# Bias rows of two MLPs in two fp32r parts inside the down passes, and attention heads begun inside the projections

## What is computed

```python
# MLP of the first block (width 4096, squared ReLU)
y = square(relu(h @ w1 + b1)) @ w2 + b2
# LRU mixer's last step
m = (h * gelu(yb)) @ w_out + b_out
# both attentions, 8 heads of 128 (+64 rotary in the first)
s = q @ k.T * scale + bias_or_mask
p = exp(s - max(s)) / sum(exp(s - max(s)))
o = p @ v
```

## Time and profile before

| | us |
|---|---|
| median of 3 runs | 1750.84 (1749.12 to 1753.19) |
| the profiled execution | 1750.2 |
| its span | 1748.6 |
| PE busy | 1646.2 (94%) |
| DVE busy | 1147.3 (66%) |
| ACT busy | 839.1 (48%) |
| POOL busy | 153.8 (9%) |
| chain that ended last, share of PE | 71% |
| the same, share of DVE | 16% |

### The profile page before, as it was taken

One profiled execution on the slowest core, in us unless ns is written; L12 is line 12 of the kernel. 1 busy time (PEld: TensorE's weight loads), 2 busy tenths in 40 slices (PEclk: granted clock), 3 DMA queues, 4 the chain that ended last, 5 costly groups with the idle time before them and its releaser, 6 DMA issues.

```text
span 1748.6 us, 20517 instructions
## 1 busy us (share of the span) xinstructions
PE 1646.2 (94%) x8221; PEld 1327.7 (76%) x8221; DVE 1147.3 (66%) x1354; ACT 839.1 (48%) x1134; POOL 153.8 (9%) x293
## 2 busy tenths in 40 slices
PE   7778999988988999999999999999999999799998
PEld 3656787875677788878888868888788888578887
DVE  4699778888969665575546876544754546665554
ACT  3553465544234555544335875334634435553433
POOL 4510100026600100000000000000000000000000
PEclk9878999999999999999999989999999999899999
DMA  9838588752036566445654554555555554245551
GB/s 305 310 126 308 185 302 332 288 214 100 1 142 220 193 227 238 161 168 192 225 184 141 199 189 171 192 192 169 207 178 183 186 188 167 96 144 193 193 191 74
DMA packets 145096, 335.45 MB, mean 192 GB/s; under 512 B 18213, under 2 KB 34061, under 8 KB 143850
## 3 DMA queue, kind: packets, MB, share of 16 engines
q1 hardware_dynamic: 134310, 293.65, 48.8%
q0 software_dynamic: 9696, 37.29, 5.6%
q10 hardware_dynamic: 996, 3.20, 0.5%
HBM read 328.86 MB, written 6.83 MB: 192 GB/s over the span
## 4 chain that ended last, share of the span: by engine, by line
PE 71%; DVE 16%; ACT 5%; issue 4%; POOL 2%; DMA 1%; SPq 1%; DVEq 0%; ACTq 0%; POOLq 0%
PE ps L670 22%; PE ps L672 22%; PE ps L671 22%; DVE wlo L1794 3%; PE ps L755 2%; ACT whi L1253 1%; DMA operands<-in_mod_mix_w 1%; PE ps L749 1%; DVE work L2247 1%; DVE xlo L1799 1%; PE ps L762 1%; DVE B L1927 1%; POOL mod L2509 1%; DVE B L1926 1%; DVE small L1859 1%
## 5 line engine op out<-in xcount | busy, mean ns | idle before, releaser
L1794 DVE TENSOR_TENSOR wlo<-raw,whi 128x2048 fp32r<-128x2048 f32 (+2 forms) x247 | 559.8, 2283 | 253.5 <-ACT whi L1253 252.2
L1253 ACT ACTIVATE whi<-raw 128x2048 fp32r<-128x2048 f32 (+2 forms) x247 | 466.9, 1908 | 233.9 <-PE ps L672 170.5
L670 PE MATMUL ps<-whi,xhi 128*128 128x512 f32 (+2 forms) x1244 | 477.5, 384 | 18.9 <-DVE xlo L1799 17.3
L672 PE MATMUL ps<-whi,xlo 128*128 128x512 f32 (+2 forms) x1244 | 471.8, 379 | 0.0
L671 PE MATMUL ps<-wlo,xhi 128*128 128x512 f32 (+2 forms) x1244 | 471.7, 379 | 0.0
L670 PE MATMUL ps<-whi,hhi 128*128 128x512 f32 x736 | 294.6, 400 | 6.2 <-DVE hlo L1799 5.2
L671 PE MATMUL ps<-wlo,hhi 128*128 128x512 f32 x736 | 289.0, 393 | 0.0
L672 PE MATMUL ps<-whi,hlo 128*128 128x512 f32 x736 | 288.8, 392 | 0.0
L670 PEld LDWEIGHTS ps<-whi,xhi 128*128 128x128 f32 x1244 | 235.5, 189 | 64.6 <-DVE xlo L1799 21.0
L672 PEld LDWEIGHTS ps<-whi,xlo 128*128 128x128 f32 x1244 | 235.5, 189 | 44.2
L671 PEld LDWEIGHTS ps<-wlo,xhi 128*128 128x128 f32 x1244 | 235.8, 190 | 41.7
(11 more groups left out here) (371 smaller groups left out, 1599.8 us busy)
## 6 DMA issues: line engine op xcount, KB each, us to landing
raw<-in_mlp_w SPq DMA_DIRECT2D x64, 1024.0 KB, 5.6
raw<-in_ffn_w_gate SPq DMA_DIRECT2D x44, 1024.0 KB, 5.1
raw<-in_ffn_w_up SPq DMA_DIRECT2D x44, 1024.0 KB, 5.2
raw<-in_ffn_w_down SPq DMA_DIRECT2D x44, 1024.0 KB, 4.9
mod<-in_mod_ffn_w POOLq DMA_DIRECT2D x16, 1024.0 KB, 6.9
mod<-in_mod_mix_w POOLq DMA_DIRECT2D x12, 1024.0 KB, 7.4
operands<-in_mod_mix_w SPq DMA_DIRECT2D x8, 1024.0 KB, 8.5
raw<-in_lru_w_in SPq DMA_DIRECT2D x8, 1024.0 KB, 5.2
```

Source lines behind the costliest of these rows:

```text
L670: pe.matmul(o, lh, rh, start=start, stop=False)
L672: return pe.matmul(o, ll, rh, start=False, stop=stop)
L1253: act.activation(whi[:, c % SPL, 0:n], raw[:, c % RAW, 0:n], ACT.Copy).then_inc(hi_done, 1)
L1794: dve.tensor_tensor(wlo[:, c % RAW, 0:n], raw[:, c % RAW, 0:n], whi[:, c % SPL, 0:n].bitcast(F32), ALU.subtract).then_inc(lo_done, 1)
```

## The change

- **MLP bias rows.** ScalarE rounds the bias row to fp32r (`brow_hi`) between `hi(c+4)` and `hi(c+5)`, VectorE makes the rest (`brow_lo`) between `lo(c+4)` and `lo(c+5)`. `open_acc` is no longer called in the MLPs: the first down pass of each token half issues, for each of its two banks, two fp32r matmuls of one row (high and low part) ahead of the first product. They come after the wait for `hid_ok`.
- **LRU.** `open_acc("lru")` stands ahead of `turned(3)` instead of behind it.
- **First attention.** Group 0's rotary transposes stand inside the projection of group 1, group 1's after the scores of head 0; the loop starts on `q_ok` 2 and `qt_ok` 1, and the waits for all of them move to i = 1. ScalarE does `hi(5)` between the two rotary copies.
- **Second attention.** The scores of heads 0 to 2 stand inside the last projection passes; ScalarE's feature copies of slice 0 go ahead of `hi(c+5)`, `hi(c+6)` between the two token copies; VectorE's `lo(c+6)` moves behind the first head.
- **Softmax weights.** In both attentions VectorE gives only the reciprocal (`recips`, signal `rc_ok`); ScalarE multiplies the weights in place, two Copy activations with a scale column, after the exponential of the next head, and gives `p_ok`.

```diff
             def down(c, tile, tt, first=False, final=False, src=(hhi, hlo), biased=None):
 ...
                     for n in range(2):
+                        if biased and k == 0:
+                            half = slice(512 * n, 512 * (n + 1))
+                            pe.matmul(ps[:, 2 * tt + n, :], ones_r[0:1, :], brow_hi[:, half], start=True, stop=False)
+                            last = pe.matmul(ps[:, 2 * tt + n, :], ones_r[0:1, :], brow_lo[biased][:, half], start=False, stop=False)
+                            if tt and n:
+                                last.then_inc(acc_open, 1)
 ...
-                    if i == 0:
-                        open_acc(name)
                     for tt in range(T):
+                        if i == 0:
+                            acc_ready(name, tt)
+                            pe.wait_ge(brow_lo_ok, MLPS.index(name) + 1)
                         pe.wait_ge(hid_ok, HID0[name] + 2 * i + tt + 1)
-                        down(mlp_down(name, i, 0), 4 * (i % 2), tt)
+                        down(mlp_down(name, i, 0), 4 * (i % 2), tt, biased=name if i == 0 else None)
 ...
                 sliced(3, 1, 9)
-                turned(3)
                 pe.wait_ge(lg_ok, KT)
                 open_acc("lru")
+                turned(3)
 ...
+                    if g:
+                        turn_rotary(0)
 ...
-                pe.wait_ge(q_ok, 4)
-                pe.wait_ge(qt_ok, 2)
+                pe.wait_ge(q_ok, 2)
+                pe.wait_ge(qt_ok, 1)
                 attention(0, qT, kT, V, True)
 ...
             def beside_attention(i):
+                if i == 0:
+                    turn_rotary(1)
                 if i == 1:
+                    pe.wait_ge(q_ok, 4)
+                    pe.wait_ge(qt_ok, 2)
                     same_step()
 ...
                 hi(c + 4)
+                if l == 0:
+                    act.activation(ones_r[:, :], ones[0:1, :], ACT.Copy)
+                act.wait_ge(brow_in, 16 * (l + 1))
+                act.activation(brow_hi[:, :], brow[name], ACT.Copy).then_inc(brow_hi_ok, 1)
                 hi(c + 5)
 ...
+                    if 1 <= i <= HEADS:
+                        s = (i - 1) % 3
+                        act.wait_ge(rc_ok, HEADS * n + i)
+                        for tt, (lo, up) in enumerate(((0, P), (P, 3 * P))):
+                            last = act.activation(sms[:, s, lo:up], sms[:, s, lo:up], ACT.Copy, scale=recips[:, 2 * s + tt:2 * s + tt + 1])
+                        last.then_inc(p_ok, 1)
 ...
                     lo(c + j)
+                    if j == 4:
+                        dve.wait_ge(brow_hi_ok, MLPS.index(name) + 1)
+                        rest(brow_lo[name][:, :], brow[name], brow_hi[:, :]).then_inc(brow_lo_ok, 1)
 ...
-                        do(dve.reciprocal(newton[:, 0:2], atts[:, 2 * s:2 * s + 2]))
-                        dve.tensor_scalar(sms[:, s, 0:P], sms[:, s, 0:P], newton[:, 0:1], None, ALU.mult)
-                        dve.tensor_scalar(sms[:, s, P:3 * P], sms[:, s, P:3 * P], newton[:, 1:2], None, ALU.mult).then_inc(p_ok, 1)
-                        dve.wait_ge(p_ok, e + 1)
+                        dve.reciprocal(recips[:, 2 * s:2 * s + 2], atts[:, 2 * s:2 * s + 2]).then_inc(rc_ok, 1)
 ...
                 c = FIRST["att"]
                 for tt in range(T):
                     token_turn("att", 0, tt)
-                for tt in range(T):
-                    project("att", c + 3, slice_bank(1, tt), tt, 1)
+                project("att", c + 3, slice_bank(1, 0), 0, 1)
+                acc_ready("att", 1)
+                pe.wait_ge(feat_ok, FEAT0["att"] + 2)
+                scores(1, 0, qT2, kT2, False)
+                scores(1, 1, qT2, kT2, False)
+                project("att", c + 3, slice_bank(1, 1), 1, 1)
+                scores(1, 2, qT2, kT2, False)
```

More of the change, by code:

```diff
@@ L965, in mla, with turn_rotary @@
                 spread_third(1, (6, 7))
+            def turn_rotary(g):
+                pe.wait_ge(qp_ok, g + 1)
+                for r in range(2):
+                    for tt in range(T):
+                        last = pe.transpose(ps[:, 4 * g + 3, r * L + tt * P:r * L + (tt + 1) * P], qp_tok[:, g, tt, r * P:(r + 1) * P], ident[:, :])
+                last.then_inc(qt_ps, 1)
             def z_pass(c, tt):
@@ L2187, in attention @@
                         piece(6)
+                    if n and i == 0:
+                        lo(FIRST["att"] + 6)
             def s5():
@@ L2361, in att @@
                 c = FIRST["att"]
-                for j in range(3, 7):
+                for j in range(3, 6):
                     lo(c + j)
```

61 lines of the change are left out of this document (34 added, 27 removed).

## The result

| | us |
|---|---|
| before, median of 4 runs | 1751.3 (1749.12 to 1753.19) |
| after, median of 4 runs | 1769.2 (1768.51 to 1771.42) |
| ratio after / before | 1.0107, 95% interval 1.0092 to 1.0123 |
| the profiled executions: before, after | 1750.2, 1768.5 |
| their spans | 1748.6, 1766.7 |

The change costs 18 us. The forecast was 1756.3, range 1749.5 to 1761.5: the sign is right, the loss is three times the forecast one, and outside the range.

The account below looks back on a forecast made before the run. TensorE, busy 94% of the span, was taken as the bound. MLPs +6.1, LRU +0.5, first attention -1.4, second +1.2, less 0.3 for slack, gave +6.1 on 1750.2: 1756.3 us, range 1749.5 to 1761.5.

Parts of the forecast that it names:

- VectorE's extra instruction: MLP starts: one more VectorE instruction for the bias row, ahead of residual, makes hid_ok come 1.22 us later.
- Idle time of 5.7: MLP starts: TensorE's idle time before the first down pass grows from 0.8 to about 5.7 us.
- LRU: LRU end: fourth down pass at most 1.4 us earlier, half clock after the wait costs 1.9; +0.5 us.
- Second attention: Second attention: ScalarE's copies lengthen the period to about 3.97 us, early scores give some back; +1.2 us.
- First attention: First attention: VectorE saves 0.6 us a head, GpSimd's slower chain costs 0.7; -1.4 us in all.
- the MLP term: Both MLP starts: later hid_ok plus bias matmuls now behind the wait, +3.04 us each, +6.1 for both.
- The price of the bias matmuls: MLP starts: eight bias matmuls each, 0.23 us apart at full clock, add 1.82 us to TensorE's path.
- The half clock: MLP starts: half clock after TensorE's restart stays at 5.8 and 2.9 us, no change, ±1.5 for each.
- One-row matmuls lower the clock: Rival, MLPs: one-row matmuls cause the half clock, so down passes start at full clock; 1752.0 us, chance 0.14.
- Early starts arrive: Rival, first attention and LRU: waits end earlier than assumed, 5.4 and 7.2 us gained; 1743.7 us, chance 0.08.
- ScalarE the bound: Rival, both attentions: ScalarE's copies cost 0.75 us and also stand in the way in the first; 1761.3 us, chance 0.12.
- GpSimd shut out: Rival, first attention: VectorE's pieces hold GpSimd's chain, memset and head 3 about 3 us later; 1758.6 us, chance 0.11.

Follow-up runs that it names:

- run 3: Changed kernel with the eight fp32r bias matmuls of each MLP moved ahead of the wait for hid_ok; 1759.49 us.
- run 6: Changed kernel with the MLP starts as before the change and the softmax weights multiplied on VectorE again in both attentions; 1754.09 us.
- run 4: Changed kernel without the eight bias matmuls of each MLP, the rounding of the bias row and the wait for it kept; 1760.61 us.
- run 5: Changed kernel with the eight one-row bias matmuls of each MLP replaced in place by eight matmuls of 128 rows; 1762.07 us.
- run 9: Changed kernel with 24 full matmuls added ahead of the first wait for hid_ok in each MLP, where TensorE idled; 1759.07 us.
- run 2: Kernel before with the MLP part of the change alone; 1765.3 us.
- 12: The combined kernel of 11 with the eight bias matmuls of each MLP back inside the passes, residual still late; 1746.2 us.
- run 1: Changed kernel with the MLP starts as before (fp32 bias matmuls ahead of the wait, no bias rounding); 1754.89 us.
- run 10: Kernel before with only VectorE's residual moved behind the two hidden steps of slice 0, bias matmuls still fp32; 1747.53 us.
- run 8: Kernel before with MLP bias rows in two fp32r parts ahead of the wait and VectorE's residual behind the hidden steps of slice 0; 1744.21 us.
- 11: Combined kernel: late residual, split bias rows ahead, first attention as changed, second with early scores but scaling on VectorE, old LRU order; 1741.55 us.
- run 7: Kernel before with only the LRU's open_acc moved ahead of the last eight transposes; 1751.22 us.

## Why the prediction was right in its sign and wrong in its size

**What held.** VectorE's extra instruction: +1.22 forecast, the gap grew by 1.30 and 1.33. Idle time of 5.7: measured 5.75 and 5.78. That the old fp32 rows were hidden and give nothing back: run 3, which hides them again, recovers 10 us. LRU: +0.5 forecast, +1.6 measured, with the wait for `hg_lo` 2 (5.11) and the half clock behind it as described. From the last projection matmul the fourth pass comes 1.4 earlier (22.51 in place of 23.87), as summed; the half clock of 6.1 us behind it costs 3.0 where the sum had 1.9. It lies at the sum's upper bound. Second attention: +1.2 forecast, +2.1 measured, period 3.97 forecast and 3.98 to 3.99 measured; the pair of copies was put at 0.6 and takes 0.69 from start to next start (1518.86 to 1519.55). Run 6 shows that all of the loss is the scaling. First attention: -1.4 forecast. It starts 0.3 later and ends 0.4 earlier in the profiled executions, -0.7. GpSimd's memset came 1.5 later in the stage where the sum had 0.7, and the scaling on ScalarE is worth about 3 (run 6), not 2.15. That the terms nearly cancel is partly luck: this stage's length varies by more than 0.7 with the same code.

**What failed: the MLP term.** The prediction put it at +3.04 each, +6.1 for both; the windows give +8.8 and +7.0, beyond its upper bound of +4.5 too. The wait of 1.22 in it was right; two steps were wrong.

- The price of the bias matmuls: "8 for each MLP, 0.23 us apart at full clock", 1.82 us. The rate was taken from products of 128 rows; at full clock the eight cost 3.3, since a change between one row and 128 slows two steps by 0.1 each. Missing: 1.5 for each, 3.0 in all. The trace of before had a hint that was passed over: from the last projection matmul (194.33) to the first bias row (194.65) it is 0.32, not 0.23.
- The half clock: "I take the same stretches after the restart, no change". Measured: 7.0 and 3.7 lost in place of 2.8 and 1.4, +6.5 in all. This is the bigger error, and it has a cause that runs 4, 5 and 9 isolate: after the same idle time the half clock costs 2.0 to 2.6 with products of 128 rows alone (four starts, runs 4 and 5) and 3.4 to 7.0 with eight single rows among them (four starts, after and run 2); with the wait filled or 0.6 to 0.8 us long it costs nothing (9, 12). Here the idle time starts it and the single rows draw it out. The medians agree in direction and give smaller sizes: after lies 8.6 us over run 4 and 7.1 over run 5, and less the bias matmuls' price (6.6, and 3.0 over 128 rows) that leaves 2.0 and 4.1 for the longer half clock.

Sum for both MLPs: 2.6 (gap) + 6.6 (bias matmuls) + 6.5 (half clock) = 15.7, against 15.8 in the windows. The stages grew by 14.4, so 1.4 is regained later in them, where the prediction took off 0.3 for slack. The half clock's part is the least certain: in run 2 the same code lost 3.8 and 3.4, 3.0 more than before in place of 6.5. By the medians the MLP part costs 13.4 (run 2 against before) to 14.3 (after against run 1).

**The range** allowed +4.5 for each MLP "if the half clock lasts longer" but did not carry both MLPs' upper ends into 1761.5, and no row set that upper end.

**The rivals.** *One-row matmuls lower the clock*: its mechanism is borne out (run 10, and the kernel before, whose clock fell ahead of the 0.8 us of waiting), its consequence was drawn the wrong way. It asked what happens when the one-row matmuls go, but the change did not remove them, it moved them to where TensorE has just restarted. The test it named, first down matmuls 0.23 apart, came out against it. *Early starts arrive*: no; both waits end where the prediction put them. *ScalarE the bound*: in the second attention only, run 6. *GpSimd shut out*: the memset came 1.5 later, between the 0.7 of the sum and the 3 of the lock. By the rule of the Trainium skill, "SBUF — State Buffer", § Who interferes with whom, the loser of the shared port stands still for the whole of the other's instruction; the rows show both slowed, a piece's instruction 2.11 in place of 1.28 on VectorE and a GpSimd one 1.92 in place of 1.06, and they do not settle how the port was granted: two engines that wait for each other by turns would show such lengths too.

## What to carry to other kernels

Before work is made cheaper inside a wait, ask what the wait is for: here `hlo` stood behind 5.2 us of VectorE work that nobody needed yet, and reordering that, with the split bias rows ahead of it (run 8), won 7 us where splitting them inside the passes lost 14. The two help each other: with the reordering alone the time can't be told from no change (run 10, -2.5 by the medians), and the split rows ahead of an unchanged wait gained nothing (run 3). Work that is hidden in a wait should stay there as long as the wait does. TensorE's long idle times cost twice, once as a wait and once as the half clock behind it, so such a stretch can be better filled than left (run 9 gained 9 to 10 us by adding matmuls). Price a matmul from a row with the same operand height and the same neighbours, and keep matmuls of one row away from a restart.

## What the runs showed of the hardware that was not expected

- **A change between one and 128 rows costs time.** Starts are 0.23 us apart within a kind and 0.33 on the steps where the kind changes and on the one behind (run 9), so a pair of one-row matmuls costs 0.88 among products and 0.47 in a row of its own (196.14 to 196.61 in run 8).
- **Matmuls of one row do not keep the clock.** After 3.6 us of them without a gap the clock was 0.52 for 3.5 us, in both MLPs (run 10). Behind the LRU's bias rows (3.7 us at full clock in after) it fell as well, again without a gap, in all eight traces with the changed order. Those are fp32; behind 1.9 us in fp32r it fell in two of four starts (the second MLP of runs 8 and 11). With full clock around them, eight of them spread over 14.3 us did no harm (runs 9 and 12).
- **The same code, two lengths.** The first attention's stage, from the first feature copy on, took 139.8 to 140.0 us in five profiled executions (after, 1, 3, 4, 5) and 142.3 to 142.7 in three (9, 11, 12), with the same instructions up to there; GpSimd's memset stands at 57.7 and at 59.7 us into it. The unchanged attention does the same: 140.5 in three (before, 8, 10), 142.2 in run 7, 143.8 in run 2. That is more than the change of that stage, and what chooses between the two is open. The half clock's length after the same idle time spreads in the same way (8.8 and 15.5 us in the first MLP), so a term of 1 to 2 us is read from several traces, not from one.
